# A third weight unit gets a raw buffer of its own and is loaded ahead of x; rounding, x transposes and stores are placed anew

## The reference

```
mn = rmsnorm(mem, g)                     # 256 memory rows x 1024
mem_k = mn @ w_mem_k                     # 1024 x 1024, kept and returned
mem_v = mn @ w_mem_v                     # 1024 x 1024, kept and returned
xn = rmsnorm(x, norm_mix_g)              # 320 rows x 1024
i_raw, f_raw = two groups of 4 columns of xn @ w_in    # the mLSTM gates
z = the other columns of xn @ w_in       # queries, keys, values, gates ...
```

## Time and profile before

| | |
|---|---|
| time, median of 3 | 860.86 us (860.27 to 861.04) |
| profiled execution | 860.39 us |
| its span | 858.6 us |
| PE busy in the span | 836.0 us (97%) |
| DVE busy | 588.8 us (69%) |
| ACT busy | 471.9 us (55%) |
| mean granted clock of TensorE | 0.988 |
| unit 1 landed; unit 2 landed | 13.6 us; 23.0 us |
| first matmul of unit 2 | 27.43 us |

### The profile page before, as it was taken

The page is one execution under the profiler, slowest core; times in us unless marked ns, Lnnn a source line. Parts: engine busy times, 40 slices in busy tenths (PEclk is TensorE's granted clock), DMA queues, the critical chain, the costliest instruction groups (busy, mean ns, idle before and its releaser), DMA issues. The chain is left out here.

```text
span 858.6 us, 12939 instructions
## 1 busy us (share of the span) xinstructions
PE 836.0 (97%) x5133; PEld 761.7 (89%) x5133; DVE 588.8 (69%) x824; ACT 471.9 (55%) x639; POOL 93.9 (11%) x153
## 2 busy tenths in 40 slices
PE   6899999999999999999999999999999999999995
PEld 6899989999988998999999999988888888888883
DVE  5656577774344546677665555868889889899893
ACT  5565467754333334454233435746778678767763
POOL 3302111020011011000000000010003111310410
PEclk9899999999999999999999999989999999999998
DMA  9747643334433334536436455479999999999960
GB/s 269 217 154 233 199 134 121 115 96 150 148 113 129 127 125 149 169 108 198 129 126 210 151 191 201 171 238 363 369 347 355 357 401 371 360 368 376 375 259 18
DMA packets 100387, 186.61 MB, mean 217 GB/s; under 512 B 5668, under 2 KB 71488, under 8 KB 100320
## 3 DMA queue, kind: packets, MB, share of 16 engines
q1 hardware_dynamic: 95280, 171.47, 58.3%
q0 software_dynamic: 4240, 12.59, 4.3%
q10 hardware_dynamic: 800, 1.66, 0.5%
HBM read 178.55 MB, written 7.93 MB: 217 GB/s over the span
## 5 line engine op out<-in xcount | busy, mean ns | idle before, releaser
L1379 DVE TENSOR_TENSOR unit_r<-arena,unit_r 128x2048 fp32r<-128x2048 f32 x63 | 144.8, 2299 | 136.5 <-ACT unit_r L989 136.3
L1388 DVE TENSOR_TENSOR w_r<-arena,w_r 128x2048 fp32r<-128x2048 f32 x96 | 216.9, 2286 | 27.7 <-ACT w_r L1000 27.7
L593 PE MATMUL pj<-xn_r,unit_r 128*128 128x320 f32 x1536 | 233.9, 311 | 0.0
L593 PEld LDWEIGHTS pj<-xn_r,unit_r 128*128 128x128 f32 x1536 | 225.5, 188 | 3.5 <-issue 3.0
L897 PE MATMUL pj<-w_r,xg 128*128 128x512 f32 x768 | 190.9, 398 | 0.2 <-ACT xg L1231 0.2
L1000 ACT ACTIVATE w_r<-arena 128x2048 fp32r<-128x2048 f32 x96 | 180.3, 1909 | 4.0 <-DMA arena<-in_w_exp_up 4.0
L897 PEld LDWEIGHTS pj<-w_r,xg 128*128 128x128 f32 x768 | 141.8, 188 | 30.9 <-issue 0.3
L989 ACT ACTIVATE unit_r<-arena 128x2048 fp32r<-128x2048 f32 x63 | 120.1, 1907 | 23.6 <-PE pj L593 20.0
L926 PE MATMUL pj<-w_r,hidT 128*128 128x512 f32 x384 | 93.3, 392 | 0.6 <-ACT hidT L1244 0.6
L926 PEld LDWEIGHTS pj<-w_r,hidT 128*128 128x128 f32 x384 | 71.8, 188 | 17.0 <-issue 0.8
L593 PE MATMUL pj<-br_r,unit_r 128*128 128x320 f32 x384 | 59.6, 311 | 0.0
(11 more groups left out here) (362 smaller groups left out, 807.6 us busy)
## 6 DMA issues: line engine op xcount, KB each, us to landing
arena<-in_w_in SPq DMA_DIRECT2D x40, 1024.0 KB, 5.3
arena<-in_w_exp_gate SPq DMA_DIRECT2D x64, 512.0 KB, 4.6
arena<-in_w_exp_up SPq DMA_DIRECT2D x64, 512.0 KB, 5.9
arena<-in_w_exp_down SPq DMA_DIRECT2D x64, 512.0 KB, 5.3
arena<-in_w_mem_v SPq DMA_DIRECT2D x4, 1024.0 KB, 5.9
arena<-in_w_br_mem SPq DMA_DIRECT2D x4, 1024.0 KB, 5.1
arena<-in_w_br_mlstm SPq DMA_DIRECT2D x4, 1024.0 KB, 5.1
arena<-in_w_br_gmlp SPq DMA_DIRECT2D x4, 1024.0 KB, 5.2
```

What stands on the lines that cost most here:

```text
L593: last = mm(bank_of(s)[0:out_rows, 0:out_cols], l, r, start=k == 0, stop=k == len(pairs) - 1)
L1379: v.tensor_tensor(unit_r[n % RING][:, 1, :], ringw[:, n % RING, :], unit_r[n % RING][:, 0, :], ALU.subtract).then_inc(u_lo, 1)
L1388: v.tensor_tensor(w_r[u % NS][:, 1, :], raw_w[u % NS], w_r[u % NS][:, 0, :], ALU.subtract).then_inc(m_lo, 1)
```

## The change

- Raw buffers: `raw_unit` has three places for the first three units: the two of the ring and 2,048 columns at `B0 + 4 * D`, which are the place of `cmk` and `cmv` later. Units from 3 on alternate between the first two again (`unit_slot`, `unit_loads`). Unit 2 lies in the third.
- Loads: SP issues unit 2 with no wait, ahead of x; unit 3 follows x and waits for the second part of unit 0 (all of it); unit 4 for that of unit 1. From unit 5 on the waits are as before.
- Rounding: units 2 and 3 are no longer rounded behind the last tile of units 0 and 1. Unit 2 is rounded at the end of `memnorm`, ahead of the evictions of memk(0, ..). Unit 3 is rounded inside `xnorm`: on ACT behind the squares of x and ahead of the evictions of memk(1, ..), on DVE behind the variance and ahead of the scaling of x.
- Steps: `xT(0)` stands behind memk(3, 0) instead of memk(2, 0), `xT(1)` and `xT(2)` both behind memk(3, 1) instead of memk(2, 1) and memk(3, 0). `gates` stays behind memv(0, 0).
- POOL: the loads behind `u_hi` = 4 wait for `u_lo` = 3 also; the stores of memory keys and values wait until `rbb` has landed.

```
@@ make_steps
-             xT(0), xT(1), xT(2), lambda: None, lambda: step("gates"), ...
+             lambda: None, lambda: None, xT(0), lambda: (xT(1)(), xT(2)()), lambda: step("gates"), ...
+def unit_slot(n):
+    return n if n < 3 else (n - 1) % RING
+def unit_loads(n):
+    return 1 if n < 3 else 2 + (n - 3) // RING
@@ buffers
-        ringw = at(RING0, RING, UW)
+        ring_raw = at(RING0, RING, UW)
+        raw_unit = [ring_raw[:, 0, :], ring_raw[:, 1, :], at(B0 + 4 * D, UW)]
-        unit_full = [sem(f"unit_full{i}") for i in range(RING)]
+        unit_full = [sem(f"unit_full{i}") for i in range(RING + 1)]
@@ SP
-                if n == RING:
+                if n == 3:
                     for i, (t0, rows_) in enumerate(TILES):
...
-                if n >= RING:
-                    sp.wait_ge(u_lo, n - RING + 1)
+                if n >= 3:
+                    sp.wait_ge(u_lo, n - 2 if n < 5 else n - 1)
@@ ACT
             def unit_first_part(n):
-                act.wait_ge(unit_full[n % RING], 16 * (n // RING + 1))
+                act.wait_ge(unit_full[unit_slot(n)], 16 * unit_loads(n))
                 if n >= RING:
                     act.wait_ge(ready["pj"], _last_use[n - RING] + 1)
...
                     af(sd[:, 3:5], var[:, 3:5], ACT.Sqrt).then_inc(s_sd, 1)
+                    unit_first_part(2)
                 elif kind == "xnorm":
                     act.wait_ge(s_x, 48)
                     for i, (t0, n) in enumerate(TILES):
                         af(xs_tm[0:n, i, :], x_tm[0:n, i, :], ACT.Square, accum_out=ssx[0:n, i:i + 1]).then_inc(s_ss, 1)
+                    unit_first_part(3)
                     act.wait_ge(s_var, 2)
...
-                elif s["ring"] == "pj" and kind != "qk" and s["last"] and s["unit"] + RING < len(UNITS):
+                elif s["ring"] == "pj" and kind != "qk" and s["last"] and 3 < s["unit"] + RING < len(UNITS):
                     unit_first_part(s["unit"] + RING)
@@ DVE
                     refine(1, 3, 5, s_rsm)
+                    unit_second_part(2)
                 elif kind == "xnorm":
...
                     v.tensor_copy(nt[:, 22:23], var[:, 0:1]).then_inc(s_var, 1)
+                    unit_second_part(3)
                     refine(2, 0, 3)
...
-                elif s["ring"] == "pj" and kind != "qk" and s["last"] and s["unit"] + RING < len(UNITS):
+                elif s["ring"] == "pj" and kind != "qk" and s["last"] and 3 < s["unit"] + RING < len(UNITS):
                     unit_second_part(s["unit"] + RING)
@@ POOL
             pool.wait_ge(u_hi, 4)
+            pool.wait_ge(u_lo, 3)
...
                     pool.wait_ge(*done("memv", 3, 1))
+                    pool.wait_ge(s_rbb, 16)
```

More of the change, by code:

```diff
@@ L89, in make_steps @@
     early = [lambda: None, lambda: step("xnorm", ring=None, eng=None), lambda: step("params"), lambda: step("state"),
-             xT(0), xT(1), xT(2), lambda: None, lambda: step("gates"), lambda: (step("gates_log", ring=None, eng=None), x_rest(0)()), x_rest(1), x_rest(2),
+             lambda: None, lambda: None, xT(0), lambda: (xT(1)(), xT(2)()), lambda: step("gates"), lambda: (step("gates_log", ring=None, eng=None), x_rest(0)()), x_rest(1), x_rest(2),
              lambda: step("gates_scan", ring=None, eng=None), lambda: step("gates_exp", ring=None, eng=None), lambda: step("wsT"), lambda: step("cols")]
@@ L554, in _ @@
                     continue
-                if n >= RING:
-                    sp.wait_ge(u_lo, n - RING + 1)
+                if n >= 3:
+                    sp.wait_ge(u_lo, n - 2 if n < 5 else n - 1)
                 src = I[name][0, :, col:col + 256].rearrange("(k p) n -> p k n", p=128)
-                sp.dma_start(ringw[:, n % RING, :].rearrange("p (k n) -> p k n", n=256), src).then_inc(unit_full[n % RING], 16)
+                sp.dma_start(raw_unit[unit_slot(n)].rearrange("p (k n) -> p k n", n=256), src).then_inc(unit_full[unit_slot(n)], 16)
                 if n == len(UNITS) - 9:
@@ L985, in unit_first_part @@
             def unit_first_part(n):
-                act.wait_ge(unit_full[n % RING], 16 * (n // RING + 1))
+                act.wait_ge(unit_full[unit_slot(n)], 16 * unit_loads(n))
                 if n >= RING:
                     act.wait_ge(ready["pj"], _last_use[n - RING] + 1)
-                af(unit_r[n % RING][:, 0, :], ringw[:, n % RING, :], ACT.Copy).then_inc(u_hi, 1)
+                af(unit_r[n % RING][:, 0, :], raw_unit[unit_slot(n)], ACT.Copy).then_inc(u_hi, 1)
             def first_unit_high(half, signal):
                 cs = slice(half * (UW // 2), half * (UW // 2) + UW // 2)
-                af(unit_r[0][:, 0, cs], ringw[:, 0, cs], ACT.Copy).then_inc(signal, 1)
+                af(unit_r[0][:, 0, cs], raw_unit[0][:, cs], ACT.Copy).then_inc(signal, 1)
             def memory_squares(i):
@@ L1378, in unit_second_part @@
                 dve.wait_ge(u_hi, n + 1)
-                v.tensor_tensor(unit_r[n % RING][:, 1, :], ringw[:, n % RING, :], unit_r[n % RING][:, 0, :], ALU.subtract).then_inc(u_lo, 1)
+                v.tensor_tensor(unit_r[n % RING][:, 1, :], raw_unit[unit_slot(n)], unit_r[n % RING][:, 0, :], ALU.subtract).then_inc(u_lo, 1)
             def rest(dst, x, high, count, value, signal):
@@ L1432, in _ @@
                             rest(mn_r[:, 1, 0:4, 0:128], mnT[:, 0:4, 0:128], mn_r[:, 0, 0:4, 0:128], s_mnh, 1, s_mnl)
-                            rest(unit_r[0][:, 1, h0], ringw[:, 0, h0], unit_r[0][:, 0, h0], u0_hi, 1, u0_lo)
+                            rest(unit_r[0][:, 1, h0], raw_unit[0][:, h0], unit_r[0][:, 0, h0], u0_hi, 1, u0_lo)
                             rest(mn_r[:, 1, 4:8, 0:128], mnT[:, 4:8, 0:128], mn_r[:, 0, 4:8, 0:128], s_mnh, 2, s_mnl)
                         else:
-                            rest(unit_r[0][:, 1, h1], ringw[:, 0, h1], unit_r[0][:, 0, h1], u_hi, 1, u_lo)
+                            rest(unit_r[0][:, 1, h1], raw_unit[0][:, h1], unit_r[0][:, 0, h1], u_hi, 1, u_lo)
                             rest(mn_r[:, 1, :, 128:256], mnT[:, :, 128:256], mn_r[:, 0, :, 128:256], s_mnh, 3, s_mnl)
```

11 lines of the change are left out of this document (8 added, 3 removed).

## The result

The changed kernel takes 868.06 us in the median (866.78 to 868.66, four runs) against 860.57 for the kernel before in the same comparison: a ratio of 1.0081, 95% interval 1.0061 to 1.0100, that is 7.0 us slower (5.2 to 8.6) by the ratio; the medians lie 7.5 apart. A second comparison gave 867.26 against 860.92, 1.0078 (1.0061 to 1.0094). The forecast was 864.0, with a range up to 865.9: the direction and the place were right, the size was not.

The account below looks back on a forecast made before the run. PE, busy 97% of the span, was taken as the bound. Gap -3.1, half clock -2.6, unit 3 late +0.4, gates stall +6.4, new half clock +2.0 gave +3.1 us: 863.5 from the profiled 860.39, 864.0 as median; range 859.6 to 865.9.

Parts of the forecast that it names:

- What unit 2 gains: PE ahead of memk(2, 0): unit 2 lands sooner, so the gap (3.1 us) and the half clock behind it (2.6) go.
- half clock -2.6: PE at memk(2, 0) and xT(0): the slow clock behind the first gap goes, saving 2.6 us.
- the 5.7: PE around unit 2: total gain claimed from the gap (3.1 us) and the half clock (2.6).
- Unit 3 late, +0.4: PE ahead of memk(3, 0): a wait of 0.4 us for unit 3's rounding, bounds 0 to 1.
- The stall at the gates, +6.4: PE ahead of the gates: waits 6.4 us for xT(2)'s eviction, which stands behind unit 5's landing and rounding.
- even with nothing else late: PE ahead of the gates: the bare row of evictions and unit 5's rounding makes it wait until 44.3, 2.5 us.
- counted from its own issue it lands at 41.6: Unit 5's load, issued at 30.6, taking 11.0 us as before; 41.9 was taken, bounds 36 and 43.2.
- The new half clock, +2.0: PE behind the stall at the gates: a new slow stretch costs 2.0 us, between 1.1 and 2.6.
- The rest and the tail: From the gates on: order unchanged, the tail shifted whole; POOL's later stores cost 0, bounds 0 to 0.3 us.
- the gap of 0.8 us: PE after 559.4 us: said to be followed by a slow stretch, 562.4 to 569.25.
- None of the four: Rivals: unit 5 in time, 0.28; gates not held by unit 5, 0.05; clock stays full, 0.1; unit 2 gains nothing, 0.04.
- Rival 1: At the gates: unit 5 lands in time, gates start at 45.6, result 859.7 to 862.0 us; chance 0.28.

Follow-up runs that it names:

- b1: The kernel before again, no edit, for another profile: 860.27 us in one execution.
- b2: The kernel before again, no edit, for a third profile: 864.80 us in one execution.
- experiment 1: The changed kernel with unit 5 rounded by ACT and DVE behind the work of xT(2): 857.10 us, ratio to the kernel before 0.9973.
- experiment 2: The changed kernel with POOL's ten loads waiting until ACT has rounded unit 5 instead of unit 3: 861.32 us, ratio to the kernel before 1.0015.
- Experiment 9: The changed kernel with unit 6's load waiting until ACT has rounded unit 5: 863.54 us in one execution.
- e6: The changed kernel again, no edit, for a second profile: 867.26 us in the median of four runs, 866.63 profiled.
- a3: The changed kernel again, no edit, for a third profile: 866.34 us in a single execution.
- experiment 5: The kernel before with only the stores of memory keys and values waiting for the spread gate rows: 860.91 us, ratio 1.0011.
- Experiment 7: The kernel before with 42 filling matmuls on PE ahead of the gates: 869.22 us against 860.92, ratio 1.0091.

## Why the prediction was right in its place and wrong in its size

**What unit 2 gains**: right in kind. Unit 2 was there when ACT came to it at 18.25, the gap at 24.3 went, and with it the slow stretch. The size was read from one execution. The term "half clock -2.6" is 1.5 in b1, b2 and the kernel with later stores (5.24 and 5.25 us for memk(2, 0) and xT(0), against 3.75), and the gap was 2.4 to 3.1. The kernel before is usually 1.2 to 2.3 us further at memv(0, 1) than the profile that the sum started from: 49.4 in the mean of the three others, against 51.14. So the 5.7 holds against that profile; in the mean of the four it is 4.6 (2.8 for the gap, 1.8 for the clock). This hid, because the slow stretch that was long at 27 us was short in the router stage of the same execution, so the profiled time of 860.39 looked like the median.

**Unit 3 late, +0.4**: it was 0 in the three profiles of the changed kernel, and 0.3 in experiment 1. x landed at 22.2, not 23.0, and unit 3 had landed by 25.4.

**The stall at the gates, +6.4**: right in its mechanism. Experiment 1 removes it by the order alone, and experiment 2 leaves the floor of 2.5 us that the prediction gave for "even with nothing else late". The first step that failed is the landing of unit 5 in this term: "counted from its own issue it lands at 41.6 ...; I take 41.9", with 43.2 as the upper bound. Unit 5 took 13.0 to 14.1 us and landed at 42.7 to 43.8; the stall was 7.6 to 8.8, 8.3 in the mean. The price of 11.0 us was the lowest of five in which the kernel before and its variants gave 11.0 to 13.7 with the same neighbours. How much of the rest comes from unit 6, issued 6.5 us behind it instead of 7.2, is not shown.

By the rule of the Trainium skill (DMA: Bandwidth & Descriptors, Queues, rings and completion order), that a DMA engine takes turns between its queues and goes through each in order, unit 5 would have landed at about 40, by the prediction's estimate. Experiment 9, without unit 6, came near it (40.7). The changed kernel did not, though SP's queue had moved 1.04 MB from 29.5 to 39 us in its first profile, nearly the bytes of a unit (some of them may be unit 6's). Which pieces landed late, and what held them, is not shown.

**The new half clock, +2.0**: the gates took 6.49, 5.87 and 5.68 us in the three profiles of the changed kernel instead of 4.06, so 1.6 to 2.4. Right in size, though the way there was another: in the first profile the clock fell 2.1 us into the gap, as in the old one, but stayed low for 10.2 us, and in e6 and a3 it fell 5.1 us into it and stayed low for 6.8.

**The rest and the tail**: "the tail is shifted whole" held up to the ranks, 509.1 to 509.2 us behind memv(0, 1) in all three profiles of the changed kernel, and experiment 5 shows no cost of the stores. Experiment 7 shows that the delay itself breeds no more. Behind the ranks it failed, and this is the second step that did: the sum gives the router stage 0, but the first profile's 9.83 us was the short one of four, and 11.3 to 11.9 is usual in both kernels. The prediction had booked the slow stretch there to the gap of 0.8 us; it came as well where there was no gap.

Together: the three profiled executions of the changed kernel take 866.6 us in the mean, 6.2 above the 860.39 that the sum started from, where it had 3.1. Of these 6.2, 4.5 are there at memv(0, 1) (55.6 against 51.14: -5.7, +8.3 for the stall and +1.9 for the half clock) and 1.7 in the router stage (11.5 against 9.83). So the two failed steps are worth 1.9 and 1.7 us, and unit 3's 0.4 that did not come goes against them.

Against the mean of four profiles for the kernel before, 49.8 and 11.3, the change costs 5.8 us at memv(0, 1) and 0.2 in the router stage. The comparisons say 7.0 (5.2 to 8.6) and 6.7, and 6.0 lies within their intervals. The median of 868.06 is 1.3 above the execution that was profiled, and no profile shows where that goes. Some executions lose time elsewhere, as b2 did; how often each kernel does, these profiles don't say.

**The rivals.** None of the four happened. Rival 1 (unit 5 in time) had the right time for its case, partly by luck: experiment 2 made that case, and its 861.32 lies within the 859.7 to 862.0 given for it. But its gates started at 43.62, not 45.6, and its router stage took 11.43 us, not 9.83. The forecast's own upper end, 865.9, was too low because unit 5's price and the router stage were each taken at one row, of an execution that had both at their lowest.

## What to carry to other kernels

In engines that work in order, a moved step takes with it everything that stands ahead of it in the lists of the other engines: ask of each moved wait which long, DMA-bound piece of work now stands between the step and its release (here 1.9 + 2.3 us of rounding for a unit that had not landed). Here the better edit was to swap two entries in those lists, not to move the step: that alone turned a loss of 7 us into a gain of 2.3 (0.2 to 4.4, by the interval). And a sum that starts from a profiled execution should check the length of its clock dips, and the landing times that it carries over, in a second profile before it books them.

## What the runs showed of the hardware that was not expected

- The stretches at the lower clock differ in length between executions of one kernel: about 3.4, 6.8, 10.2 and 13.7 us were seen, 3.4 or 6.8 behind the same gap in the kernel before. At full or half clock 24 matmuls are 3.11 or 5.5 us, so the same gap costs 1.5 or 2.6 us more. One followed a gap of 2.4 us (b1), and in the router stage one began with no gap ahead of it.
- A window of the clock reads 1.00 where the trace has no record of it. In the kernel before the first record begins at 12.9 us; the first 10 us show 1.00, but there the transposes of 128x128 take 1.97 us for eight, against 1.03 for eight of the same form at 36.76, so PE ran at the lower clock. The Trainium skill (TensorE: Matmul & The Clock Gate, What's actually happening) calls the throttled state the default; these rows agree.

```profile
5.26 1.97 PE L692 MATMUL ms<-ident,arena 128*128 128x128 f32 x8 [2.10 <-DMA arena<-in_mem_prompt]
```

- A load of 1 MB in pieces of 1 KB took 5.0 to 5.4 us with none of POOL's loads beside it, and 11.0 to 14.2 beside ten smaller ones; the same loads at the same distances gave anything from 11.0 to 13.7. In one profile 0.16 MB in pieces of 16 and 128 bytes slowed it as much as 1.5 MB in larger ones.
